# Attention values of two heads at a time, transposed as they are computed, in a two-layer hybrid encoder on Trainium2

## What is computed

```python
def reference(...):
    for l in range(DEPTH):
        h = rmsnorm(x, norm1_g[l])
        proj = h @ w_in[l]
        aq, ak, av, bq, bk, bv, cq, ck, cv = jnp.split(proj, splits, axis=-1)
        out_a = mixer_chunked_relbias(...)
        out_b = mixer_swa_sinks(...)
        out_c = mixer_diff(...)
        mixed = jnp.concatenate([out_a, out_b, out_c], axis=-1)
        x = x + mixed @ w_out[l]
        h2 = rmsnorm(x, norm2_g[l])
        x = x + jnp.square(jax.nn.relu(h2 @ w_up[l])) @ w_down[l]
    return x
```

## Time and profile before

| | us |
|---|---|
| median of 3 runs (2161.3 to 2163.95) | 2162.88 |
| profiled execution | 2162.83 |
| its span, first to last instruction | 2161.0 |
| mixing stage of layer 0, steps 13 to 83 | 263.55 |
| the same of layer 1 | 263.50 |
| PE busy / DVE / ACT / POOL in the span | 2106.8 / 1270.2 / 1021.2 / 197.5 |
| granted TensorE clock, mean | 0.995 |

### The profile page before, as it was taken

The page is one execution under the profiler, slowest core; times in us unless marked ns, Lnnn a source line. Parts: engine busy times, 40 slices in busy tenths (PEclk is TensorE's granted clock), DMA queues, the critical chain, the costliest instruction groups (busy, mean ns, idle before and its releaser), DMA issues.

```text
span 2161.0 us, 26782 instructions
## 1 busy us (share of the span) xinstructions
PE 2106.8 (97%) x10742; PEld 1773.0 (82%) x10742; DVE 1270.2 (59%) x1531; ACT 1021.2 (47%) x1389; POOL 197.5 (9%) x205
## 2 busy tenths in 40 slices
PE   7999999999999999999999989999999999999999
PEld 6777778888888888888878777888888888888887
DVE  6576446665556565556666664465655655565566
ACT  5456654443444344344445566544434434443444
POOL 2444120000000000000034421000000000000000
PEclk9999999999999999999999999999999999999999
DMA  7565676666666666666656566766666666666664
GB/s 261 153 186 151 162 184 195 187 189 195 189 191 192 191 190 189 194 189 191 185 175 189 150 156 161 206 180 185 192 192 191 187 195 193 186 194 193 187 193 149
DMA packets 209388, 400.72 MB, mean 185 GB/s; under 512 B 14862, under 2 KB 21872, under 8 KB 209264
## 3 DMA queue, kind: packets, MB, share of 16 engines
q1 hardware_dynamic: 203856, 381.85, 59.7%
q0 software_dynamic: 4608, 16.78, 4.1%
q10 hardware_dynamic: 800, 0.37, 0.1%
HBM read 380.05 MB, written 2.12 MB: 177 GB/s over the span
## 4 chain that ended last, share of the span: by engine, by line
PE 90%; ACT 4%; DVE 2%; POOL 2%; issue 1%; DMA 1%; SPq 0%; DVEq 0%; ACTq 0%
PE psum L476 22%; PE psum L440 18%; PE psum L442 18%; PE psum L441 18%; PE psum L479 11%; ACT w_hi L628 2%; PE psum L486 2%; DVE w_lo L801 1%; ACT w_lo L630 1%; DMA x<-in_x_dram 1%; DVE panel L927 0%; PE psum L550 0%; PE psum L537 0%; PE psum L535 0%; POOL head_in L1139 0%
## 5 line engine op out<-in xcount | busy, mean ns | idle before, releaser
L801 DVE TENSOR_TENSOR w_lo<-raw_ring,w_hi 128x1024 fp32r<-128x1024 f32 (+1 forms) x692 | 851.6, 1231 | 791.4 <-ACT w_hi L628 791.3
L628 ACT CAST w_hi<-raw_ring 128x1024 fp32r<-128x1024 f32 (+1 forms) x724 | 753.6, 1041 | 996.3 <-PE psum L442 601.6
L476 PE MATMUL psum<-xt,w_hi 128*128 128x512 f32 x2048 | 512.9, 392 | 0.0
L440 PE MATMUL psum<-w_hi,ht_hi 128*128 128x512 f32 x1280 | 503.8, 394 | 0.0
L442 PE MATMUL psum<-w_hi,ht_lo 128*128 128x512 f32 x1280 | 499.4, 390 | 0.0
L441 PE MATMUL psum<-w_lo,ht_hi 128*128 128x512 f32 x1280 | 499.3, 390 | 0.0
L476 PEld LDWEIGHTS psum<-xt,w_hi 128*128 128x128 f32 x2048 | 368.8, 189 | 66.3
L479 PEld LDWEIGHTS psum<-xt,w_lo 128*128 128x128 f32 x2048 | 279.4, 190 | 20.0
L479 PE MATMUL psum<-xt,w_lo 128*128 128x256 f32 x2048 | 285.5, 282 | 0.0
L440 PEld LDWEIGHTS psum<-w_hi,ht_hi 128*128 128x128 f32 x1280 | 241.1, 188 | 50.7 <-issue 2.0
L442 PEld LDWEIGHTS psum<-w_hi,ht_lo 128*128 128x128 f32 x1280 | 240.9, 188 | 50.8
(11 more groups left out here) (121 smaller groups left out, 1157.2 us busy)
## 6 DMA issues: line engine op xcount, KB each, us to landing
raw_ring<-in_w_up_dram SPq DMA_DIRECT2D x256, 512.0 KB, 3.7
raw_ring<-in_w_down_dram SPq DMA_DIRECT2D x256, 512.0 KB, 3.6
raw_ring<-in_w_in_dram SPq DMA_DIRECT2D x132, 512.0 KB, 4.0
raw_ring<-in_w_out_dram SPq DMA_DIRECT2D x64, 512.0 KB, 4.5
w_lo<-raw_ring POOLq DMA_DIRECT2D x32, 512.0 KB, 4.6
raw_ring<-in_w_in_dram SPq DMA_DIRECT2D x16, 256.0 KB, 2.8
x<-in_x_dram SPq DMA_DIRECT2D x4, 512.0 KB, 9.9
out_dram<-x SPq DMA_DIRECT2D x4, 512.0 KB, 4.8
```

The lines of the kernel that those rows point to most:

```text
L440: pe.matmul(out_ap, t_hi, m_hi, start=start, stop=False, skip_group_check=True)
L476: pe.matmul(bank[:, f, :], w_hi[:, w, j, f * P:(f + 1) * P], both, start=kt == 0, stop=False, skip_group_check=True)
L628: act.copy(w_hi[:, u % AHEAD, :, 0:cols], raw_ring[:, u % RAWS, :, 0:cols]).then_inc(hi_ready, 1)
L801: dve.tensor_tensor(w_lo[:, u % AHEAD, :, 0:cols], raw_ring[:, u % RAWS, :, 0:cols], w_hi[:, u % AHEAD, :, 0:cols].bitcast(F32), ALU.subtr ...
```

## The change

The tables are laid out anew: scores of C come at 25, 29, 33, 37 (before 24, 31, 35, 39), of A at 71 to 77 (before 69 to 75), those of B stay. The T groups of q and k move a step or two back, and the normalization always stands in the step of its T group. `post_c` part 0 moves from step 51 to 46 and part 1 from 55 to 56, and POOL's root for it stands before Bq1 instead of behind it.

For B and A (pairs 4 to 15) DVE divides the probabilities in a new function `weight`, at the third step after the scores, before PE transposes them. Then V stands in the array, head 0 on columns 0 to 63 and head 1 on columns 64 to 127, and the transposed probabilities move, 256 and then 128 columns. The result is the transposed value of both heads, 128 partitions by 256 rows of x, which is one of the 16 operands of the output projection: ACT casts it straight into `ht` hi, DVE subtracts into `ht` lo (`pair_lo`). The six T groups "mix", their panels and casts and the six quarters are left out; the T groups "mixC" for the C heads stay. A third buffer for `probs_t` comes in.

```diff
-PAIR_AT = {**{s: h for h, s in enumerate((24, 31, 35, 39))}, **{49 + 2 * n: 4 + n for n in range(8)}, **{69 + 2 * n: 12 + n for n in range(4)}}
+PAIR_AT = {**{25 + 4 * h: h for h in range(4)}, **{49 + 2 * n: 4 + n for n in range(8)}, **{71 + 2 * n: 12 + n for n in range(4)}}
-COMBINE = {32: 0, 35: 1, 39: 2, 43: 3}
+COMBINE = {s + 4: n for s, n in PAIR_AT.items() if n < 4}
+WEIGHT = {s + 3: n for s, n in PAIR_AT.items() if n >= 4}
-PROBS_T = {**{s: h for h, s in enumerate((33, 37, 41, 45))}, **{51 + j: 4 + j for j in range(16)}, **{71 + j: 20 + j for j in range(8)}}
-VALUES = {s + 2: f for s, f in PROBS_T.items()}
-POST_C = {51: 0, 55: 1}
+PROBS_T = {**{s + 5: n for s, n in PAIR_AT.items() if n < 4},
+           **{s + 3 + m: 2 * n - 4 + m for s, n in PAIR_AT.items() if n >= 4 for m in range(2)}}
+VALUES = {s + (7 if n < 4 else 5): n for s, n in PAIR_AT.items()}
+MIXES = len(VALUES)
+POST_C = {46: 0, 56: 1}
-T_USE = {**{n + 2: ("x1", 5 + n) for n in range(3)}, 13: ("qk", 0, 0), 14: ("qk", 0, 1), 22: ("qk", 1, 0), 23: ("qk", 1, 1),
-         38: ("qk", 3, 0), 45: ("qk", 4, 0), 46: ("qk", 4, 1), 55: ("mixC", 6), 56: ("mixC", 7), 53: ("qk", 5, 0),
-         54: ("qk", 5, 1), 58: ("mix", 2), 59: ("qk", 6, 0), 60: ("qk", 6, 1), 62: ("mix", 3), 66: ("mix", 4),
-         67: ("qk", 7, 0), 68: ("qk", 7, 1), 70: ("mix", 5), 79: ("mix", 0), 82: ("mix", 1)}
+T_USE = {**{n + 2: ("x1", 5 + n) for n in range(3)}, 14: ("qk", 0, 0), 15: ("qk", 0, 1), 23: ("qk", 1, 0), 24: ("qk", 1, 1),
+         39: ("qk", 3, 0), 46: ("qk", 4, 0), 47: ("qk", 4, 1), 53: ("qk", 5, 0), 55: ("qk", 5, 1), 57: ("mixC", 6),
+         59: ("qk", 6, 0), 61: ("qk", 6, 1), 65: ("mixC", 7), 67: ("qk", 7, 0), 69: ("qk", 7, 1)}
-NORM_STEP = {0: 13, 1: 22, 3: 38, 4: 45, 5: 53, 6: 58, 7: 66}
+NORM_AT = {s: use[1:] for s, use in T_USE.items() if use[0] == "qk"}
...
@@ transpose_probs
-                    pe.wait_ge(exped, pl.at(JOBS, j + 1))
+                    pe.wait_ge(weighted, pl.at(PAIRS - 4, (f - 4) // 2 + 1))
...
@@ values
+                pe.wait_ge(pt_copied, pl.at(FILLS, f + (2 if n < 4 else 3)))
+                pe.wait_ge(pv_copied, pl.at(MIXES, n + 1))
                 pe.wait_ge(t_free, pl.at(T_USES, T_BEFORE + sum(t < s for t in T_STEPS)))
...
+                for m in range(2):
+                    if n < 12:
+                        v = [v_b[:, t, (n - 4) // 4 * HD:((n - 4) // 4 + 1) * HD] for t in range(RT)]
+                    else:
+                        v = [v_ca[:, t, (2 * (n - 12) + m) * HD:(2 * (n - 12) + m + 1) * HD] for t in range(RT)]
+                    heads.append((ps_v[m * HD:(m + 1) * HD, :], v, probs_t[:, (f + m) % 3, :]))
+                for o, v, t in heads:
+                    pe.matmul(o[:, 0:2 * P], v[0], t[:, 0:2 * P], start=True, stop=False, skip_group_check=True)
+                for o, v, t in heads:
+                    mm = pe.matmul(o[:, P:2 * P], v[1], t[:, 2 * P:3 * P], start=False, stop=True, skip_group_check=True)
+                mm.then_inc(pv_ready, 1)
...
@@ copy_values
+                    act.copy(ht[0][:, n % 12, :], ps_v[:, 0:SEQ]).then_inc(pair_hi, 1)
...
@@ DVE
+            def weight(pl, n):
+                j = 2 * n
+                dve.wait_ge(exped, pl.at(JOBS, j + 2))
+                den = sums[:, j:j + 2, :]
+                if n < 12:
+                    link(dve.tensor_tensor(den, den, sink_e[:, j - 8:j - 6, :], ALU.add))
+                f = small[:, 3, 0:4]
+                link(dve.reciprocal(f.rearrange("p (m r) -> p m r", m=2), den))
+                for m in range(2):
+                    p = probs[:, (j + m) % 4, :]
+                    for r, (lo, hi) in enumerate(((0, P), (P, 3 * P))):
+                        last = dve.tensor_scalar(p[:, lo:hi], p[:, lo:hi], f[:, 2 * m + r:2 * m + r + 1], None, ALU.mult)
+                last.then_inc(weighted, 1)
+            def pair_lo(pl, n):
+                dve.wait_ge(pair_hi, pl.at(PAIRS - 4, n - 3))
+                dve.tensor_tensor(ht[1][:, n % 12, :], ps_v[:, 0:SEQ], ht[0][:, n % 12, :].bitcast(F32), ALU.subtract).then_inc(pv_copied, 1)
...
                 if s in POST_C:
                     post_c(pl, POST_C[s])
+                if s in WEIGHT:
+                    weight(pl, WEIGHT[s])
                 if s in STATS_AT:
                     head_sums(pl, STATS_AT[s])
                 if s in NORM_AT:
                     head_norm(pl, *NORM_AT[s])
-                if s in QUARTERS:
-                    quarter(pl, QUARTERS[s])
...
+                if s in VALUES and VALUES[s] >= 4:
+                    pair_lo(pl, VALUES[s])
...
@@ POOL
+                    if c == 5:
+                        pool.wait_ge(c_summed, pl.l + 1)
+                        rsqrt(small[:, 7, 0:8], small[:, 6, 0:8], 8, 1.0 / P, 2).then_inc(c_rstd, 1)
```

More of the change, by code:

```diff
@@ L114 @@
 PANELS_BEFORE = 5
[L115 removed]
+PANEL_OF_MIX = {T_USE[s][1]: n for n, s in enumerate(PANEL_STEPS) if T_USE[s][0] == "mixC"}
 FIRST_X2 = min(n for n, s in enumerate(PANEL_STEPS) if T_USE[s][0] == "x2")
[L117 to L119 removed]
+NORM_AT = {s: use[1:] for s, use in T_USE.items() if use[0] == "qk"}
 STATS_AT = {8 * c + 7 + 1: c for c in QK}
@@ L176, in encoder @@
         probs = sb("probs", [P, 4, 3 * P])
-        probs_t = sb("probs_t", [P, 2, 3 * P])
+        probs_t = sb("probs_t", [P, 3, 3 * P])
         rows = probs_t[0:ROWS, 0, 0:P]
         junk = probs_t[:, :, :].rearrange("p s n -> p (s n)")[:, 0:CW]
-        mixed = sb("mixed", [P, 3, CW])
+        mixed = sb("mixed", [P, RT, CW])
         panel = sb("panel", [P, 2, 2, SEQ])
@@ L238, in encoder @@
         pv_copied = sem("pv_copied")
+        pair_hi = sem("pair_hi")
+        weighted = sem("weighted")
         mix_ready = sem("mix_ready")
@@ L500, in use_t @@
                         blocks = [head_in[:, use[2] * CW + b * P:use[2] * CW + (b + 1) * P] for b in range(4)]
-                elif use[0] in ("mix", "mixC"):
+                elif use[0] == "mixC":
                     k = use[1]
[L503 to L508, removed]
+                    pe.wait_ge(mix_ready, pl.l + 1)
+                    blocks = [mixed[:, r, b * P:(b + 1) * P] for b in (2 * (k - 6), 2 * (k - 6) + 1) for r in range(RT)]
                 else:
@@ L518, in use_t @@
                 pe.wait_ge(t_free, pl.at(T_USES, T_BEFORE + T_NUMBER[s]))
-                pe.wait_ge(pv_copied, pl.at(FILLS, 1 + sum(v <= s for v in VALUES)))
+                pe.wait_ge(pv_copied, pl.at(MIXES, 1 + sum(v <= s for v in VALUES)))
                 transposes(blocks)
@@ L524, in scores @@
                 if n < 4:
-                    q, k, b, kb, ready = qk_t[0], qk_t[1], n, n, 23
+                    q, k, b, kb, ready = qk_t[0], qk_t[1], n, n, 24
                 elif n < 12:
                     g, b = divmod(n - 4, 4)
-                    q, k, kb, ready = (qk_t[1] if g else qk_t[2]), kb_t, g, (54 if g else 46)
+                    q, k, kb, ready = (qk_t[1] if g else qk_t[2]), kb_t, g, (55 if g else 47)
                 else:
-                    q, k, b, kb, ready = qk_t[0], qk_t[1], n - 12, n - 12, 68
+                    q, k, b, kb, ready = qk_t[0], qk_t[1], n - 12, n - 12, 69
                 pe.wait_ge(t_free, pl.at(T_USES, T_BEFORE + T_NUMBER[ready] + 1))
@@ L551, in transpose_probs, with values @@
                 mm.then_inc(pt_ready, 1)
[L553 to L560, removed]
+            def values(pl, s, n):
+                f = n if n < 4 else 2 * n - 4
+                chunk = 2 if n < 4 else 3 if n < 12 else 8
@@ L567, in values @@
-                pe.matmul(o[:, dv:2 * dv], t[:, P:2 * P], v[0], start=True, stop=False)
-                pe.matmul(o[:, dv:2 * dv], t[:, 2 * P:3 * P], v[1], start=False, stop=True).then_inc(pv_ready, 1)
+                if n < 4:
+                    v, t = [v_ca[:, t, n * P:(n + 1) * P] for t in range(RT)], probs_t[:, f % 3, :]
+                    pe.matmul(ps_v[:, 0:P], t[:, 0:P], v[0], start=True, stop=True)
+                    pe.matmul(ps_v[:, P:2 * P], t[:, P:2 * P], v[0], start=True, stop=False)
+                    pe.matmul(ps_v[:, P:2 * P], t[:, 2 * P:3 * P], v[1], start=False, stop=True).then_inc(pv_ready, 1)
+                    return
@@ new lines, in values @@
+                heads = []
+                for m in range(2):
[6 more added lines that the diff above has]
+                    pe.matmul(o[:, 0:2 * P], v[0], t[:, 0:2 * P], start=True, stop=False, skip_group_check=True)
@@ L576, in mix @@
                 else:
-                    pe.wait_ge(panel_done, pl.at(PANELS, PANELS_BEFORE + PANEL_OF_MIX[k] + 1))
+                    if k >= 6:
+                        pe.wait_ge(panel_done, pl.at(PANELS, PANELS_BEFORE + PANEL_OF_MIX[k] + 1))
+                    else:
+                        pe.wait_ge(pv_copied, pl.at(MIXES, (2 * k + 1 if k >= 2 else 2 * k + 13) + 2))
                     rows_unit(pl, s, ht, (2 * k, 2 * k + 1), chunk, k == PAIRS_CB[0], k == PAIRS_A[1], cols)
@@ L701, in exponentials, with copy_values @@
```

(14 more changed lines are left out.)

14 lines of the change are left out of this document (3 added, 11 removed).

## The result

The changed kernel takes 2125.07 us (median of 4 runs, 2122.87 to 2126.12) against 2162.74 in the same session: ratio 0.9822, 95% interval 0.981 to 0.9833. Forecast were 2123.

The account below looks back on a forecast made before the run. PE, busy 90% of the chain, was taken as the bound, plus its holes and clock. Per layer 5.3 us of PE's work and 14.5 of holes and clock go, 19.8; 39.6 in all, 2162.9 to 2123 us; range 2109 to 2149.

Parts of the forecast that it names:

- PE's work: Steps 13 to 83: six mixed-value transpose groups removed (2.7 us), values of 24 heads as 12 pairs (2.6): 5.3 us per layer.
- The halves: Values of a pair: two heads overlap in column halves, 1.0 us a pair; rival, in series, 7.8 more per layer, 2139, chance 0.14.
- (a): The 12 PE waits for ACT's value copy go, since T groups and values stand in different steps: 9.4 us per layer.
- (b): Cq's T groups, now at 14 and 15, meet ready rotated heads: of 2.7 us waits 1.8 go, 0.9 stays.
- (c): Waits at 45 (2.0 us, late DVE) and 52 (2.2, behind post_c's reductions, then slow clock) go; reductions move to 46.
- (d): New wait at step 46: eight reductions ahead of the normalization PE stands for, 2.2 us plus 0.8 for the clock.
- (e): Steps 25 to 34: masks and a combine among narrow units make PE wait 0.2 us at 30 and 0.9 at 32.
- (f): New weight step, 1.5 us on DVE, covered by 0.9 in pairs with values; at step 52 PE waits 1.0.
- The rival that called the change slower: Weight step bounds every pair, products at the disturbed rate, 3.7 us: 28 us per layer more, 2179 us, chance 0.08.
- (g): Steps 56 to 58 carry post_c's second half, Aq's sums and a panel: 1.0 us of waiting.
- Left over: Holes and clock remaining per layer in steps 13 to 83: 8.5 us of 23.
- The holes only move: Rival: the same 23 us per layer come back at other semaphores, only PE's 5.3 us gained: 2152 us, chance 0.10.

Follow-up runs that it names:

- e8: Changed kernel with both heads of a pair computed in the same half of the array (columns 0 to 63): 2135.92 us, ratio 0.9873.
- e5: Changed kernel with five T groups (57, 59, 61, 65, 67) one step later, in steps that hold values: 2151.64 us, ratio 0.9941.
- e6: Kernel before with the eight reductions of post_c at step 48 instead of 51: 2156.78 us, ratio 0.9968.
- e9: e2 plus the first normalization of Cq, Ck, Bkv and Bq0 one DVE step ahead of its T group: 2119.81 us, ratio 0.98.
- e10: e9 plus e3's signal per head and the first C head's values at step 33 instead of 32: 2115.11 us, ratio 0.9773.
- e3: Changed kernel with the weight step signalling PE after each head's two products instead of after all four: 2125.21 us, ratio 0.9821.
- e1: Changed kernel with a pair's value matmuls ordered head by head instead of alternating: 2125.88 us, ratio 0.9818.
- e7: Kernel before with only Cq's T groups and their normalizations one step later (14 and 15): 2160.15 us, ratio 0.9989.
- e2: Changed kernel with the eight reductions of post_c put behind the head normalization in DVE's step 46: 2120.9 us, ratio 0.9799.

## Why the prediction was right, point by point

The total: 2125.1 for 2123. The stretch gave 20.6 and 21.4 us in the two layers for 19.8, more than forecast, and yet the kernel gained 37.7 for 39.6: steps 84 and 85, behind the stretch, took 1.8 more in the two layers together, and the profiled execution is the fastest of the four, 2.2 below their median. The mechanisms came as named; that the total is as close as this is in part luck, for PE's work gave more than its term and a wait that was not foreseen took some of it back.

- **PE's work, 5.3 forecast.** What is left of the gain without idle time and clock is 7.2 us in layer 0 (20.6 less 10.0 of idle and 3.4 of clock) and 6.9 in layer 1 (21.4 less 9.4 and 5.1). The clock is read in 6 us around each place where it fell; the first line is of the kernel before, the second of the changed one:

```profile
254.00:260.00 6.00, 4.59 (x15) 3.84 (x16) 0.00 (x0) 1.96 (x4) 0.85 (x1) 0.72 0.79 211
156.00:162.00 6.00, 4.74 (x17) 3.91 (x18) 2.95 (x9) 0.65 (x2) 3.08 (x2) 0.72 0.60 175
```

  That is (1 - 0.72) x 6 = 1.7 us each time, three times in each layer before (behind the waits at 52, 67 and 79) and once after, in layer 0 alone. The term that was mis-sized is the pair's: it takes 0.89, not 1.0, so the values saved 24 x 0.61 - 12 x 0.89 = 4.0 instead of 2.6. A T group of mixed values was worth 0.63 in the steps, not 0.45: step 62 before took 4.87 us (228.12 to 232.98) and step 64, the same without it, 3.74 (237.73 to 241.47); 1.13 less the 0.50 of idle that the row shows. But 0.16 of it is the wait's own: idle counts from the modelled end of the last matmul, shown 0.27 long where the next can start after 0.11. The two terms make 4.0 + 3.7 = 7.7, some 0.6 more than was measured; where that went the steps don't single out.
- **The halves** overlap, shown by e8; in one half each pair costs 0.64 more, as the rival priced it (0.65). With that rival the kernel would still have been faster, 2135.9. The Trainium skill, TensorE: Matmul & The Clock Gate, Packing small matmuls, says that column tiles run as row tiles do; the trace agrees, with starts some 0.01 us apart. The Trainium skill, TensorEngine Tiling (Array Packing), Key Properties, tells of a drain; the trace has a gap of 0.09 us on entry.
- **(a) Copies of values.** All 12 waits went, 9.4 us, and with the two of 1.8 (steps 67 and 79) the low clock behind each, 3.4 more. That is the largest part of the gain. e5 shows what the same layout would cost with pairs; moving the T groups alone, without pairs, was not tried.
- **(b) Cq.** Forecast 0.9 left at step 14; 1.4 in layer 0, 2.0 in layer 1. Beside POOL's rotation of Cq the normalization took 1.77 us in layer 0, for 0.68 undisturbed, and in layer 1 the split ahead of it 2.36 and the normalization 1.21. At 23, 0.9 was forecast and no wait came: the split ahead is of a narrow unit (0.88 us), and POOL was through before the normalization; 0.2 came at 24.
- **(c), (d) The reductions.** e6 gives the whole of their price before (4.0 us in layer 0); in the changed kernel step 46 waited 2.3 for 2.2. The clock behind it cost 1.4 in layer 0 and nothing in layer 1, 0.8 was taken. One condition was read from the old timing: POOL was to be through with Bq0 before unit 46 began. The changed kernel reaches that unit 2.4 us earlier (152.04), and POOL ended at 153.82, 1.0 before the first reduction. So they ran undisturbed by a narrower margin than the prediction reckoned with.
- **(e)** 0.3 and 0.85 at steps 30 and 32 for 0.2 and 0.9 (by starts; the row's 0.7 is idle).
- **(f) Weight.** 1.6 at step 52 for 1.0, no wait in plain pairs. The four products took 2.17 us there beside POOL, and 0.93 at step 56, where 1.1 was forecast. The rival that called the change slower took 3.7 us for a disturbed weight step; it would be some 2.6 by step 52, and 3.2 by the slowest one seen, e9's.
- **(g)** 0.7 at step 58 for 1.0.
- **Left over:** 8.1 idle and 1.7 of clock in layer 0, 8.6 and none in layer 1, for 8.5. **Not foreseen:** the DMA wait at unit 85 of layer 1, 1.2 us in this execution, and in other runs up to 2.5. "The holes only move" holds for 15, 47, 52 and 84 once the first ones are closed (e9, e10), but not for the twelve copies and the reductions, which were most of it.

## What to carry to other kernels

Before counting what an operation costs, ask which two users of one PSUM bank stand in the same step: here twelve waits of half a microsecond to two, and 27 us if five T groups go back into the steps of values. On an engine that works in order, put what the bound engine waits for first and what only it itself needs last: ahead of a normalization the same eight reductions made PE wait 1.7 us longer (2.3 for 0.6), behind it step 47 grew by 0.2. Two products with 64 outputs took 0.89 us in two halves of the array, in either order of issue, and 1.53 in one; the results come out transposed for the next product if the small operand stands.

## What the runs showed of the hardware

- The same eight reductions of 128x128 take 746 ns each on the mean beside POOL's rotations and 280 ns at a step where POOL is idle: groups by line of the kernel before, then of the changed one.

```profile
L927 DVE CUSTOM_DVE_ANT_0 panel<-mixed 128x128 f32<-128x128 f32 x16 | 11.0, 746 | 0.0
```

```profile
L931 DVE CUSTOM_DVE_ANT_0 panel<-mixed 128x128 f32<-128x128 f32 x16 | 3.5, 280 | 0.0
```

Of the eight in layer 0 of the first, five take 0.73 to 0.75 us from start to start, one 1.29 and two 0.21; in the second all take 0.21. The Trainium skill, SBUF — State Buffer, SBUF: two separate sides, says that VectorE and GpSimd share one pair of ports, held as an exclusive lock for a whole instruction; these rows agree in sign, the page has no figure for such a pair of instructions. That the ports are the reason was not tried by itself.

- A hole of about 2 us is followed by TensorE's lower level (1.2 of 2.4 GHz) in some executions and not in others. The changed kernel had a granted clock of 1.00 around step 14 and 0.89 around step 46, e3 the other way round; at 14 they waited 1.4 and 2.0 us, at 46 both 2.3. First the changed kernel, then e3:

```profile
57.00:72.00 15.00, 13.58 (x64) 11.02 (x63) 8.70 (x8) 7.75 (x11) 9.52 (x7) 1.00 0.39 114
150.00:165.00 15.00, 12.66 (x54) 10.18 (x53) 7.95 (x22) 5.64 (x9) 6.75 (x6) 0.89 0.49 140
```

```profile
57.00:72.00 15.00, 13.01 (x55) 10.38 (x54) 8.60 (x7) 5.51 (x7) 8.52 (x7) 0.89 0.37 113
150.00:165.00 15.00, 12.66 (x63) 10.31 (x62) 8.71 (x23) 6.02 (x9) 8.96 (x7) 1.00 0.58 174
```

Each such event costs 1.4 to 1.6 us, as much as the parts of the change under test; a gain of under 3 us had to be read from the steps and not from the median. In the traces of the changed kernel and of e1 to e5, e7 and e8 the T group of step 14 started 2.38 us after the matmul ahead of it in ten layers, and six of these were followed by the lower level; it started 1.81 us after it in six, and none was. In the six of these runs that wait 2.34 us at step 46 (all but e2 and e7), the lower level followed in eight of twelve layers.
- When the stretch got shorter, the accumulating DMAs took longer to land (median 4.6 us before, 5.5 after), and PE waited for one, which it never did in the kernel before. Why they land later was not tried.
